# Turning the class block of the probabilities on VectorE instead of TensorE

## The reference, cut to what matters

```
s = einsum('brhnqe,brhnke->brhnqk', qb, kw) * HEAD_DIM**-0.5
s = where(mask, s, -inf)
m = max(s, axis=-1, keepdims=True)
p = exp(s - m);  denom = sum(p, axis=-1, keepdims=True)
o = einsum('brhnqk,brhnke->brhnqe', p, vw) / denom
```

## Time and profile before

| | us |
|---|---|
| median of 3 runs | 878.21 |
| the profiled execution | 877.4 |
| its span, first to last instruction | 875.6 |
| attention, first scores of pair 0 to the end of the last values | 258.9 to 401.0 |
| TensorE busy | 867.7 |
| VectorE busy | 457.2 |
| ScalarE busy | 322.8 |
| GpSimd busy | 151.7 |

### The profile page before, as it was taken

The page is one execution under the profiler, slowest core; times in us unless marked ns, Lnnn a source line. Parts: engine busy times, 40 slices in busy tenths (PEclk is TensorE's granted clock), DMA queues, the critical chain, the costliest instruction groups (busy, mean ns, idle before and its releaser), DMA issues.

```text
span 875.6 us, 13174 instructions
## 1 busy us (share of the span) xinstructions
PE 867.7 (99%) x4627; PEld 715.1 (82%) x4627; DVE 457.2 (52%) x638; ACT 322.8 (37%) x488; POOL 151.7 (17%) x207
## 2 busy tenths in 40 slices
PE   9999999999999999999999999999999999999998
PEld 7788788888887878878887888888888888888886
DVE  5558976677924543544686553333333334433334
ACT  6312343323246665656333343222222222322221
POOL 3789995000020000001220230000000000000000
PEclk9999999999999999999999999999999999999999
DMA  8439237534465453412725332332333332222222
GB/s 304 144 106 231 79 126 155 205 127 144 127 203 184 142 154 94 134 48 76 188 102 192 97 97 96 97 96 96 96 96 96 96 96 96 96 97 96 96 72 96
DMA packets 86082, 108.82 MB, mean 124 GB/s; under 512 B 10688, under 2 KB 51888, under 8 KB 85920
## 3 DMA queue, kind: packets, MB, share of 16 engines
q1 hardware_dynamic: 79136, 94.24, 33.6%
q10 hardware_dynamic: 5504, 10.52, 3.7%
q0 software_dynamic: 1408, 3.61, 1.8%
HBM read 94.38 MB, written 13.96 MB: 124 GB/s over the span
## 4 chain that ended last, share of the span: by engine, by line
PE 53%; DVE 1%; issue 0%; ACT 0%; ACTq 0%
PE ps L1524 27%; PE ps L1554 13%; PE ps L1249 12%; DVE late L1231 1%; DVE late L1151 0%; DVE hT_lo L1157 0%; PE ps L1443 0%; PE ps L1429 0%; DVE w_lo L558 0%; ACT w_hi L552 0%; PE ps L1539 0%; DVE late L1154 0%; PE ps L1534 0%; PE ps L1419 0%; PE ps L1415 0%
## 5 line engine op out<-in xcount | busy, mean ns | idle before, releaser
L558 DVE TENSOR_TENSOR w_lo<-w_raw,w_hi 128x1024 fp32r<-128x1024 f32 x141 | 178.2, 1264 | 318.8 <-ACT w_hi L552 318.6
L552 ACT ACTIVATE w_hi<-w_raw 128x1024 fp32r<-128x1024 f32 x141 | 149.3, 1059 | 397.0 <-PE ps L1249 162.8
L1524 PE MATMUL ps<-h_hi,w_hi 128*128 128x512 f32 x352 | 137.2, 390 | 0.0
L1524 PE MATMUL ps<-h_hi,w_lo 128*128 128x512 f32 x352 | 137.0, 389 | 0.0
L1524 PE MATMUL ps<-h_lo,w_hi 128*128 128x512 f32 x352 | 136.9, 389 | 0.0
L1249 PE MATMUL ps<-w_hi,hT_hi 128*128 128x512 f32 x280 | 109.8, 392 | 1.9 <-DVE w_lo L558 1.2
L1249 PE MATMUL ps<-w_hi,hT_lo 128*128 128x512 f32 x280 | 109.0, 389 | 0.0
L1249 PE MATMUL ps<-w_lo,hT_hi 128*128 128x512 f32 x280 | 109.0, 389 | 0.0
L415 POOL TENSOR_TENSOR early<-early 128x16 f32<-128x16 f32 (+6 forms) x129 | 91.3, 708 | 23.2 <-ACT early L575 13.2
L1249 PE MATMUL ps<-hT_hi,w_hi 128*128 128x512 f32 x224 | 91.4, 408 | 0.0
L1249 PE MATMUL ps<-hT_hi,w_lo 128*128 128x512 f32 x224 | 87.7, 391 | 0.0
(11 more groups left out here) (212 smaller groups left out, 1101.9 us busy)
## 6 DMA issues: line engine op xcount, KB each, us to landing
w_raw<-in_w_in SPq DMA_DIRECT2D x108, 256.0 KB, 3.5
w_raw<-in_w_ffn_gate SPq DMA_DIRECT2D x44, 256.0 KB, 2.8
w_raw<-in_w_ffn_up SPq DMA_DIRECT2D x44, 256.0 KB, 3.0
w_raw<-in_w_ffn_down SPq DMA_DIRECT2D x44, 256.0 KB, 2.7
z_d<-early ACTq DMA_DIRECT2D x7, 1024.0 KB, 4.9
late<-z_d SPq DMA_DIRECT2D x96, 64.0 KB
w_raw<-in_w_out SPq DMA_DIRECT2D x16, 256.0 KB, 2.8
late<-z_d SPq DMA_DIRECT2D x12, 256.0 KB
```

Of the source, the lines that this page charges most:

```text
L552: nc.scalar.activation(w_hi[:, j % WSPL], w_raw[:, j % WRAW], ACT.Copy).then_inc(w_hi_done, 1)
L558: nc.vector.tensor_tensor(w_lo[:, j % WSPL], w_raw[:, j % WRAW], w_hi[:, j % WSPL].bitcast(F32), ALU.subtract).then_inc(w_lo_done, 1)
L1524: ins = T.matmul(ps[:, m], (w_hi, w_lo)[b][:, j % WSPL, at_w:at_w + P], (h2_hi, h2_lo)[a][:, 2 * j + h, :], start=j == 0 and h == 0 and k ...
```

## The change: what it does

The fourth transpose of each unit is taken out of `turn_prob`, and ScalarE's copy out of PSUM ends at column 384. VectorE gets `turn_class`: one transpose of 32x32 blocks, 128 partitions by 128 columns, straight from `prob` to `probT` in SBUF, with a semaphore of its own, `class_turned`. It stands in VectorE's step `u` behind everything but the three `gate_out` of step 8, and turns unit `u - 1`. Three readers wait for the new semaphore: the exponentials (the buffer `prob` is free), `values` (the operand is there), and the sigmoids at the end of a pair.

```diff
@@ scalar engine
                             if u >= 2:
-                                act.wait_ge(prob_turned, 8 * i + u - 1)
+                                wait_apart(act, (prob_turned, 8 * i + u - 1), (class_turned, 8 * i + u - 1))
...
-                            nc.scalar.activation(probT[:, v % 4, k0:512], ps[:, 6, k0:512], ACT.Copy).then_inc(misc_act, 1)
+                            nc.scalar.activation(probT[:, v % 4, k0:384], ps[:, 6, k0:384], ACT.Copy).then_inc(misc_act, 1)
...
+                    act.wait_ge(class_turned, 8 * i + 8)
                     for m in range(4):
@@ vector engine
+            def turn_class(i, v):
+
+                dve.wait_ge(prob_done, 8 * i + v + 1)
+                if v >= 4:
+                    dve.wait_ge(o_done, 4 * i + v // 2 - 1)
+                V.transpose(probT[:, v % 4, 384:512], prob[:, v % 2, 384:512]).then_inc(class_turned, 1)
...
                         if u in (1, 4, 7):
                             lo(W_GATE + u // 3 + 2 + 4 * i, u // 3 + 2)
+                        if 1 <= u < 9:
+                            turn_class(i, u - 1)
                         if u == 8:
                             for m in range(3):
                                 gate_out(i, m)
@@ tensor engine
-                for x in range(0 if u // 2 else 1, 4):
+                for x in range(0 if u // 2 else 1, 3):
                     ins = T.transpose(ps[:, 6, x * P:(x + 1) * P], prob[:, u % 2, x * P:(x + 1) * P], ident[:, :])
                 ins.then_inc(prob_turned, 1)
...
                 pe.wait_ge(misc_act, MA_Y + ma_probT(2 * n + 1) + MA_PAIR * i)
+                pe.wait_ge(class_turned, 8 * i + 2 * n + 2)
```

More of the change, by code:

```diff
@@ L224, in build @@
             sem("qk_turned"), sem("scores_done"), sem("prob_done"), sem("prob_turned"), sem("o_done"))
+        class_turned = sem("class_turned")
         stats_done, stats_out, stats_in = sem("stats_done"), sem("stats_out"), sem("stats_in")
```

## The result

The changed kernel takes 879.55 us against 877.63 before (medians of 22 runs each; 879.03 to 880.38 for the changed one). The ratio is 1.0018, with a 95% interval of 1.0012 to 1.0025: slower by 0.2%, right at the bound of 1.8 us that the prediction took for what can be told from no change. The difference of the medians is 1.9 us, as forecast; the level of both is lower than the three runs of before had shown, so that 880.1 was 0.55 too high.

A forecast was written before the change was run, and what follows sets the result against it. TensorE, busy for 99% of the span, was taken to bound the kernel. Savings of 0.33 and 0.22 against waits of 0.50 and 0.53 made +0.48 a pair, +1.9 us: 878.2 to 880.1 us, range 877.9 to 882.8.

The forecast's parts named there:

- TensorE's time at the end of the attention is passed on whole: TensorE, 99% busy, ends the chain; its change between first scores and last values becomes the kernel's change in time.
- A transpose is worth 0.11 to TensorE: Each of 32 transposes removed from TensorE saves 0.11 us, 3.5 us in all if nothing else changed.
- 0.154 of busy share: Rejected price of a TensorE transpose, 18.5 / 120 us, said to count the latency tail once for each group.
- A: From scores(2) to the next gate-product piece: TensorE waits 1.5 us at values(1) for turn_class(3); 0.50 us longer a pair.
- B: End of the pair: values(3) waits for turn_class(7), behind lo and turn_class(6); 0.53 us longer a pair.
- the release: Time from the end of VectorE's transpose to TensorE's waiting values matmul: 0.20 us taken, bounds 0.06 and 0.30.
- What is hidden: turn_class(0), (1), (2), (4) and (5) on VectorE fit into idle or covered time; 0.21 us each if cover went.
- `wait_apart` at the exponentials adds nothing: ScalarE's new wait ahead of exp costs between nothing and 0.3 us; taken as nothing, since ScalarE idles ahead of exp(4).
- The sum: For a pair -0.33, +0.50, -0.22 and +0.53 make +0.48 us; four pairs +1.9 us, slower by 0.22%.
- the pure saving: Rival: nothing waits and 3.5 us go, 874.7 us; chance 0.08.
- the cheap wait: Rival: TensorE waits at both places, transpose and release at lower bounds; +0.08 a pair, 878.5 us; chance 0.30.
- the dear one: Rival: transpose 0.42 holding the next 0.35, release 0.30, 0.3 at exp(4); +1.32 a pair, 883.5 us; chance 0.18.

The follow-up runs named there:

- e5: Kernel before with only the removal: no fourth transpose, copy ends at column 384, no transpose on VectorE, values reads another block; 874.41 us against 877.93.
- e7: Changed kernel with VectorE doing the transposes of units 0, 1, 2, 4 and 5 twice; 879.44 us against 879.50 for the changed kernel.
- e2: Changed kernel with turn_class of units 0 to 5 ahead of lo, and turn_class(6) and (7) in step 7 ahead of add_o(2); 874.75 us.
- e1: Changed kernel with turn_class ahead of the lo of steps 1, 4 and 7 in VectorE's order; 876.53 us, 1.4 under before.
- e9: Kernel before with VectorE's lo of step 4 moved behind reduce(5), nothing of the change; 874.48 us, 3.5 less than before.
- e6: Changed kernel with the waits of values reordered, register values first, so the first weight load should carry the class_turned wait; 878.66 us.
- e10: Changed kernel with VectorE doing the transposes of units 3, 6 and 7 twice; 881.85 us against 877.44 before.

## Why the prediction was right

- *TensorE's time at the end of the attention is passed on whole.* It was: 142.1 to 144.1 in the attention, 1.9 at the chain's next row, 1.9 in the medians. One reading behind it was too wide: the chain of before reaches back only to 390.50, in the last pair, and not over the second half of the attention. That the other pairs pass their time on as well is shown by the four equal pairs in every trace and by the sum.
- *A transpose is worth 0.11 to TensorE.* e5 shows it: 3.5 us for 32. The 0.154 of busy share would have been 4.9.
- *The two stretches.* A was to be 0.50 longer and is 0.53 longer; B was to be 0.53 longer and is 0.53 longer. In A the transpose starts 0.22 ahead of reduce(5) and takes 0.30 (I had 0.21 and 0.32), and the release takes 0.24, 391.13 - 390.89 (I had 0.20, and it is the term whose bounds, 0.06 to 0.30, were the widest that mattered). In B the transposes are done 0.04 earlier than forecast and the release is 0.04 longer, so that the exact hit there is two errors that cancel. And 0.20 was a pick between two rows and worked out from neither; that it came within 0.04 is in part luck, for at the lower bounds the kernel would have come out as no change, a case that had a chance of 0.30. The idle times, 1.47 and 0.57, are those forecast (1.5 and 0.6).
- *What is hidden.* turn_class(0), (1), (2), (4) and (5) cost nothing that the runs can see, and e7 shows that there was room for a second one in each place. The room ahead of reduce(4) was read rightly: of 0.45 idle, 0.32 are left with one transpose, part of it spent on the next instruction's own waits.
- *`wait_apart` at the exponentials adds nothing.* reduce(4) ends at 386.93 (386.85 + 0.08), exp(4) starts at 386.96, 0.03 later. The reason is the one that was given, ScalarE's idle time: the trace has its register operation at 384.19 and its wait for the class block at 385.87, both long over by then.
- *The sum.* -0.33 + 0.53 - 0.22 + 0.53 = +0.51 a pair, +2.0 us, against the 1.9 measured. The chance for "slower" was only 0.47, against 0.45 for "same": that TensorE would wait at both places had 0.92 (all but the pure saving), but on which side of 0.2% the sum would fall was left nearly even.

Of the rivals, the cheap wait is refuted by the release of 0.24, the dear one by the transpose's 0.30 with 0.22 behind it and by exp(4), and the pure saving holds only once the queue is reordered (e2). With the ratio's interval of +1.1 to +2.2 us, whether the change is slower by over or under 0.2% stays open; that it is slower does not. Not settled either is the last few tenths between kernels: the differences of medians and of TensorE's attention agree only to about 0.5 us (e1: -1.4 and -1.0).

## What to carry to other kernels

Moving work from a full engine to a half-idle one is worth what the queue order of the second leaves of it: place the moved instruction behind the last thing that it needs, not behind the last thing in its step, and look for what stands ahead of it that waits for a third engine. Price the removed work by the distance between starts, and each new wait by the time at which its signal comes in the trace of before; here the first could be read to a hundredth without running the change and the time of the signal to a few hundredths; the release behind it could only be bounded, between 0.06 and 0.30. And where a trace shows the bound engine waiting a few tenths for a chain, the cure may be the same reordering: e9 won 3.5 us with one line moved, as much as the change could have won at best (e5).

## What the runs showed of the hardware that I had not expected

Where a wait stands among its neighbours decides what it costs once it is the last one: at values(1) TensorE started 0.05 us behind the end of the transpose when the weight load itself carried the wait (e6), and 0.24 behind when another wait's value was computed after it (the changed kernel); at values(3), where e6 still computes one, it was 0.23. And what a STREAM_TRANSPOSE takes depends on what stands ahead of it. Right behind another one it is 0.27 long with 0.19 to the next start; behind a `lo` it is 0.30 with 0.23 (e10, from the starts 392.49, 392.72 and 392.91); behind a copy out of PSUM it is 0.28 (the first row of e7 above). Why was not tested:

```profile
392.49 0.30 DVE L1049 STREAM_TRANSPOSE late<-late 128x128 f32<-128x128 f32 x1
392.72 0.27 DVE L1050 STREAM_TRANSPOSE late<-late 128x128 f32<-128x128 f32 x1
392.91 0.38 DVE L1071 CUSTOM_DVE_ANT_0 late<-ps,masks 128x256 f32<-128x256 f32 x1
```
